# Splitting two stretches of small sample matmuls, a deeper ring of value pages, and finer waits at the first tiles of W_O and W_out

## What is computed

```python
def run_layer(x, c, mix, w_ada, b_ada, g_norm1, w_in, b_forget, g_qa, g_ka, g_qb, g_kb,
              w_o_a, w_o_b, w_out, g_norm2, w_up, w_down):
    mod = (jax.nn.silu(c) @ w_ada + b_ada)[:, None, :]
    shift1, scale1, gate1, shift2, scale2, gate2 = jnp.split(mod, 6, axis=-1)
    h = rms_norm(x, g_norm1) * (1.0 + scale1) + shift1
    qa, ka, va, qb, kb, vb, qi, ki, wi, logf, ga, gb = project(h, w_in, b_forget, g_qa, g_ka, g_qb, g_kb)
    oa, ob = mix(qa, ka, va, qb, kb, vb, qi, ki, wi, logf)
    merged = (jax.nn.sigmoid(ga) * (oa.reshape(B, T, WIDTH_A) @ w_o_a)
              + jax.nn.sigmoid(gb) * (ob.reshape(B, T, WIDTH_B) @ w_o_b))
    x = x + gate1 * (merged @ w_out)
    h2 = rms_norm(x, g_norm2) * (1.0 + scale2) + shift2
    x = x + gate2 * (jnp.square(jax.nn.relu(h2 @ w_up)) @ w_down)
```

```python
    ki_all = jnp.concatenate([paged_rows(cache_k_idx), ki], axis=1)
    scores = index_scores(qi, wi, ki_all, qpos, kpos)
    _, sel = lax.top_k(scores, topk_count(L))
    oa = sparse_attend(qa, gather_selected(cache_k_a, ka, sel), gather_selected(cache_v_a, va, sel), qpos, sel)
```

## Time and profile before

| | |
|---|---|
| median of 3 runs | 951.53 us (951.21 to 955.5) |
| the profiled execution | 950.35 us, its span 948.5 us |
| PE (TensorE matmul) busy | 928.5 us, 98% of the span |
| VectorE, ScalarE, GpSimd busy | 494.1, 396.2, 140.7 us |
| mean granted TensorE clock | 0.994 of full speed |

### The profile page before, as it was taken

One profiled execution on the slowest core, in us unless ns is written; L12 is line 12 of the kernel. 1 busy time (PEld: TensorE's weight loads), 2 busy tenths in 40 slices (PEclk: granted clock), 3 DMA queues, 4 the chain that ended last, 5 costly groups with the idle time before them and its releaser, 6 DMA issues.

```text
span 948.5 us, 19876 instructions
## 1 busy us (share of the span) xinstructions
PE 928.5 (98%) x7554; PEld 852.3 (90%) x7554; DVE 494.1 (52%) x1178; ACT 396.2 (42%) x829; POOL 140.7 (15%) x140
## 2 busy tenths in 40 slices
PE   8999999999999999999999999999999999999997
PEld 7797678787878878997799999999999999999997
DVE  3654678873646797731167576444333344443332
ACT  3354556654756766333233344344211133441111
POOL 4100223222236664200000000000000000000000
PEclk9999999999999999999999999999999999999999
DMA  9648655345325563967233512333323333322212
GB/s 320 212 126 238 188 193 178 91 146 187 106 63 163 166 183 117 294 214 226 76 90 89 157 47 63 88 92 89 89 88 88 91 92 98 96 89 89 88 45 91
DMA packets 176233, 124.54 MB, mean 131 GB/s; under 512 B 14739, under 2 KB 152019, under 8 KB 176164
## 3 DMA queue, kind: packets, MB, share of 16 engines
q1 hardware_dynamic: 176034, 123.50, 43.2%
q10 hardware_dynamic: 130, 0.10, 0.0%
HBM read 116.99 MB, written 6.59 MB: 130 GB/s over the span
## 4 chain that ended last, share of the span: by engine, by line
PE 85%; DVE 5%; issue 4%; ACT 2%; DMA 1%; POOL 1%; SPq 0%; POOLq 0%; ACTq 0%; DVEq 0%
PE bank L975 24%; PE bank L976 23%; PE bank L977 23%; PE bank L1086 2%; PE bank L1063 2%; PE bank L1042 2%; PE bank L1072 2%; PE bank L881 2%; DMA vbuf<-in_cache_v_a 1%; PE bank L1104 1%; PE bank L899 1%; PE bank L1048 1%; PE bank L1127 1%; DVE sel L2006 1%; PE bank L1117 1%
## 5 line engine op out<-in xcount | busy, mean ns | idle before, releaser
L975 PE MATMUL bank<-h_hi,w_hi 128*128 128x256 f32 (+1 forms) x1232 | 359.6, 292 | 1.2 <-issue 0.6
L976 PE MATMUL bank<-h_lo,w_hi 128*128 128x256 f32 (+1 forms) x1232 | 350.2, 284 | 0.0
L977 PE MATMUL bank<-h_hi,w_lo 128*128 128x256 f32 (+1 forms) x1232 | 349.5, 284 | 0.0
L975 PEld LDWEIGHTS bank<-h_hi,w_hi 128*128 128x128 f32 x1232 | 234.2, 190 | 23.7 <-issue 18.9
L976 PEld LDWEIGHTS bank<-h_lo,w_hi 128*128 128x128 f32 x1232 | 234.1, 190 | 0.0
L977 PEld LDWEIGHTS bank<-h_hi,w_lo 128*128 128x128 f32 x1232 | 233.6, 190 | 0.0
L975 PE MATMUL bank<-u_hi,w_hi 128*128 128x264 f32 (+1 forms) x512 | 145.2, 284 | 0.0
L976 PE MATMUL bank<-u_lo,w_hi 128*128 128x264 f32 (+1 forms) x512 | 144.9, 283 | 0.0
L977 PE MATMUL bank<-u_hi,w_lo 128*128 128x264 f32 (+1 forms) x512 | 144.8, 283 | 0.0
L2423 DVE TENSOR_TENSOR w_lo<-raw,w_hi 128x1024 fp32r<-128x1024 f32 x58 | 71.1, 1226 | 132.9 <-ACT w_hi L1762 132.9
L1762 ACT ACTIVATE w_hi<-raw 128x1024 fp32r<-128x1024 f32 x58 | 61.3, 1057 | 139.8 <-PE bank L977 139.8
(11 more groups left out here) (328 smaller groups left out, 1379.0 us busy)
## 6 DMA issues: line engine op xcount, KB each, us to landing
raw<-in_w_in SPq DMA_DIRECT2D x44, 512.0 KB, 4.2
part<-in_w_ada SPq DMA_DIRECT2D x32, 512.0 KB, 5.4
raw<-in_w_up SPq DMA_DIRECT2D x32, 512.0 KB, 4.1
raw<-in_w_down SPq DMA_DIRECT2D x32, 512.0 KB, 4.1
ada<-in_w_ada SPq DMA_DIRECT2D x4, 2048.0 KB, 13.7
kv<-in_cache_k_b SPq DMA_DIRECT2D x16, 256.0 KB, 4.1
qbc<-q_d SPq DMA_DIRECT2D x16, 256.0 KB, 4.5
kv<-in_cache_k_a SPq DMA_DIRECT2D x16, 256.0 KB, 4.4
```

What stands on the lines that cost most here:

```text
L975: mm(out, hi[:, k, :], x_h, start=first and k == ks[0], stop=False)
L976: mm(out, hi[:, k, :], x_l, start=False, stop=False)
L977: end = mm(out, lo[:, k, :], x_h, start=False, stop=last and k == ks[-1])
```

## The change

Five edits. The 16 products of the samples' indexer are cut in two: eight (`first_samples`) stay at slot (3, 6), eight move with `side_step(4)` to slot (3, 7). The ring of value buffers grows from six to eight; the two new ones lie behind everything else that is allocated, fills 6 and 7 wait for nothing, and the fills move in SyncE's program. `sample_outputs` is cut in two: chunks 0 and 1 before the first half of gate tile 15, chunks 2 and 3 between its halves. The first half of the first W_O tile waits only for the first half's evacuation. The first W_out tile waits for chunk 7 only ahead of chunk 7.

```diff
-        (3, 6), (4, 7),
+        (3, 7), (4, 7),
...
-                for j, v_at in enumerate((dist_at, dist_at + 4096, at, at + 4096, at + 8192, kv0_at))]
+                for j, v_at in enumerate((dist_at, dist_at + 4096, at, at + 4096, at + 8192, kv0_at, place["at"], place["at"] + 4096))]
...
-                elif v >= 6:
-                    sp.wait_ge(pv_used, (v - 6) // 4 + 1)
+                elif v >= 8:
+                    sp.wait_ge(pv_used, v // 4 - 1)
                 m, b = batch_unit(v)
-                load_pages(vbuf[v % 6], "cache_v_", m, b, val_landed[v % 6])
+                load_pages(vbuf[v % 8], "cache_v_", m, b, val_landed[v % 8])
...
             load(T_GATE + 14)
+            load_values(6)
+            load_values(7)
             load(T_GATE + 15)
-            for v in range(6, 10):
+            for v in range(8, 12):
                 load_values(v)
             load(T_WO)
-            for v in range(10, 14):
+            for v in range(12, 2 * NS):
                 load_values(v)
             load(T_WO + 1)
             load(T_WO + 2)
-            for v in range(14, 2 * NS):
-                load_values(v)
...
+            def first_samples(p):
+
+                pe.wait_ge(side_read, 4)
+                pe.wait_ge(tok_read, 2 * p + 2)
+                pe.wait_ge(qzs_ready, 1)
+                for i in range(NS * NPAGE // 2):
+                    mm(bank[2][:, H * i:H * i + H], ki_pt[:, i, :], qzs[:, i // 2].rearrange("p c h -> p (c h)"),
+                       start=True, stop=True)
...
                 elif e == 4:
-                    pe.wait_ge(side_read, 4)
-                    pe.wait_ge(qzs_ready, 1)
-                    for i in range(NS * NPAGE):
+                    for i in range(NS * NPAGE // 2, NS * NPAGE):
...
+                if (p, s) == slot_before(*SIDE[4]):
+                    first_samples(p)
...
                 if i == T_GATE + 15:
-                    sample_outputs()
+                    sample_outputs((0, 1))
                 project(i, 0)
+                if i == T_GATE + 15:
+                    sample_outputs((2, 3))
                 project(i, 1)
...
-            pe.wait_ge(os_hi, 1)
-            pe.wait_ge(os_lo, 1)
-            pe.wait_ge(act_evac, act_evac_value(T_WO - 1, 1))
             for g in range(NCH):
...
                 for half in range(2):
+                    if g == 0:
+                        pe.wait_ge(act_evac, act_evac_value(T_WO - 1, half))
+                        if half == 1:
+                            pe.wait_ge(os_hi, 1)
+                            pe.wait_ge(os_lo, 1)
...
+                    out = out_bank(j)[:, 0:CUT[half + 1] - CUT[half]]
+                    if m == 0:
+                        pe.wait_ge(mf_hi, 2 * NCH - 3 + half)
+                        pe.wait_ge(mf_lo, 2 * NCH - 3 + half)
+                        half_tile(i, half, out, range(NCH - 1), last=False)
+                        pe.wait_ge(mf_hi, 2 * NCH - 1 + half)
+                        pe.wait_ge(mf_lo, 2 * NCH - 1 + half)
+                        half_tile(i, half, out, [NCH - 1], first=False).then_inc(proj_done, 1)
+                    else:
+                        half_tile(i, half, out).then_inc(proj_done, 1)
```

More of the change, by code:

```diff
@@ L266, in layer @@
         vbuf = [sb(f"vbuf{j}", [P, NPAGE, SEQ], F32, v_at)[0]
-                for j, v_at in enumerate((dist_at, dist_at + 4096, at, at + 4096, at + 8192, kv0_at))]
+                for j, v_at in enumerate((dist_at, dist_at + 4096, at, at + 4096, at + 8192, kv0_at, place["at"], place["at"] + 4096))]
+        assert place["at"] + 8192 <= nc.sbuf_usable_end
         assert dist_at + 8192 <= abias_at and at + 12288 <= padb_at + 8192
@@ L428, in layer @@
         qbc_landed = [sem("qbc_landed0"), sem("qbc_landed1")]
-        val_landed = [sem(f"val_landed{i}") for i in range(6)]
+        val_landed = [sem(f"val_landed{i}") for i in range(8)]
         prod_pool = sem("prod_pool")
@@ L1249, in sample_values, with sample_outputs @@
                         if pg == 0:
-                            pe.wait_ge(val_landed[v % 6], 16 * NPAGE * (v // 6 + 1))
-                        last = mm(bank[3][32 * j:32 * j + 32, :], ptz[:, 4 * pg + j, 32 * t:32 * t + 32], vbuf[v % 6][:, pg, :],
+                            pe.wait_ge(val_landed[v % 8], 16 * NPAGE * (v // 8 + 1))
+                        last = mm(bank[3][32 * j:32 * j + 32, :], ptz[:, 4 * pg + j, 32 * t:32 * t + 32], vbuf[v % 8][:, pg, :],
                                   start=t == 0 and pg == 0, stop=t == 3 and pg == NPAGE - 1)
                 last.then_inc(pv_used, 1)
-            def sample_outputs():
+            def sample_outputs(cs):
                 pe.wait_ge(om_ready, 2)
-                for c in range(4):
+                for c in cs:
                     out = bank[6][:, 256 + 2 * NS * c:256 + 2 * NS * (c + 1)]
@@ L1263, in sample_outputs @@
                                   start=False, stop=m == 1)
-                last.then_inc(os_done, 1)
+                if c == 3:
+                    last.then_inc(os_done, 1)
             for i in range(T_GATE + 5, T_WO):
@@ L1298, in _ @@
                     i, j = T_WO + NCH + m, NCH * half + m
-                    if m == 0:
-                        pe.wait_ge(mf_hi, 2 * NCH - 1 + half)
-                        pe.wait_ge(mf_lo, 2 * NCH - 1 + half)
                     if half == 0:
@@ L1305, in _ @@
                     pe.wait_ge(dve_evac, 2 * NCH + (j - 3 if j >= 4 else -2 if j < 2 else 0))
-                    half_tile(i, half, out_bank(j)[:, 0:CUT[half + 1] - CUT[half]]).then_inc(proj_done, 1)
+                    out = out_bank(j)[:, 0:CUT[half + 1] - CUT[half]]
[8 more added lines that the diff above has]
+                        half_tile(i, half, out).then_inc(proj_done, 1)
                     if (half, m) == (1, 0):
```

## The result

| | median us | lowest | highest | executions | mean granted clock |
|---|---|---|---|---|---|
| before | 951.99 | 950.42 | 955.50 | 6 | 0.990 to 0.996 |
| after | 943.87 | 939.24 | 945.64 | 6 | 0.995 to 1.000 |

The ratio is 0.9909, with a 95% interval of 0.9891 to 0.9927: faster by 0.9%, 8.1 us by the medians. The forecast was 940.5 us in a range of 937.5 to 944.7, faster. The direction and the range hold; the median lies 3.4 us above the point. (The clocks of before are those of 51 further executions, run beside the experiments.)

The account below looks back on a forecast made before the run. The PE, busy 928.5 of 948.5 us, was taken as the bound, losing time to two clock falls and value-page waits. Terms of 11.07 us gave 939.3 from the profiled 950.35, plus 1.18 for a median: 940.5 us, range 937.5 to 944.7.

Parts of the forecast that it names:

- The products in two slots: Sixteen 8-column products, cut into two stretches of 1.78 us: the clock no longer falls behind them, saving 3.27 us.
- The weakest step: At the split products: a light stretch of 1.78 us keeps the clock, though nothing between 1.95 and 3.34 us was tested.
- `sample_outputs` in two: Around gate tile 15: halves of 1.67 us keep the clock, the half tile behind takes 2.92 us, saving 1.55.
- The ring of eight: Value batches: no wait for pages, each 1.85 us from start to next tile, saving 5.75 us, at least 2.9.
- First W_O tile: Start of W_O: its first half no longer waits for the evacuation of the half just finished, saving 0.80 us.
- W_out: First W_out tile: the relaxed wait costs nothing now, so it saves 0.
- the base: Whole kernel: 1.18 us, the median's distance above the profiled execution, added to 939.3 for a median of 940.5 us.
- the sum: All terms, 3.27 + 5.75 + 1.55 + 0.80 - 0.30 = 11.07 us saved, chance 0.62.
- the upper bounds: Whole kernel: every term at its best, said to be 0.4 us better than the sum.
- The clock falls once more: Rival: a split products or outputs stretch still loses the clock, 942.1 to 943.8 us, chance 0.15; both places 945.3, 0.07.
- Four falls where there were two: Rival: each of four split stretches brings the clock down for 6.83 us; 954.1 us, slower by 0.3%, chance 0.02.
- The ring no longer waits: Answers the rival that one page pair of a value batch is late, losing 2.9 of 5.75 us: 943.4, chance 0.07.

Follow-up runs that it names:

- filled kernels: Kernels with unneeded identity matmuls put into two PE gaps, at 20.4 us and in slot (7, 6); medians from 939.5 to 949.7 us.
- whole_products: After with the sixteen products back in one slot, (3, 6); median 945.09 us, ratio 0.9932.
- add_light8: After with eight 8-column identity matmuls added between the halves of each of gate tiles 10 to 14; median 950.44 us.
- whole_outputs: After with the twelve small matmuls of `sample_outputs` in one piece again before gate tile 15; median 944.32 us, ratio 0.9908.
- ring_only: Before with the ring of eight value pages and nothing else changed; median 948.04 us, ratio 0.9943.
- held_before: Before with identity matmuls filling the PE gaps at 20.4 us and in slot (7, 6); median 949.7 us, ratio 0.9978.
- held_old_wo: held with the old wait, for both halves' evacuation, ahead of the first W_O tile; median 942.77 us.
- held_old_wout: held with the old wait ahead of the first W_out tile; median 940.56 us.
- held: After with six identity matmuls in the PE gap at 20.4 us and seven in slot (7, 6); median 939.5 us, ratio 0.9859.

## Why the prediction was right, and where it was off

**The products in two slots: right.** Both halves take 1.81 us (forecast 1.8) at 1.00. Put back, the fall is back, and the kernel is 3.1 us slower by the medians (3.27 forecast), 3.2 by the means of filled kernels, each with some 2.5 us of play. The price itself varies: 3.27 goes with a fall of 6.83 us, and the fall in the trace of whole_products lasted half of that. The weakest step, that a light stretch of 1.78 us keeps the clock, is borne out by the nine traces with split products; add_light8 has it for 1.70 us. The neighbour has its number now: 2.59 us fails in two of five places.

**`sample_outputs` in two: right in kind, the size varies.** 1.55 us was taken from a fall of 3.42 us. It may last 6.8 (whole_outputs, ring_only), for which twice that is an estimate; undone, the split costs 2.4 us by the medians, give or take 2.5.

**The ring of eight: right.** Every batch takes 1.85 us, no wait of the PE names a value page, and alone the ring gives 4.9 us by the medians, 5.5 by the means. The term of 5.75 was one execution's; held_before's has 4.40.

**First W_O tile 0.80, W_out 0: right**, by the starts in after, held_old_wo and held_old_wout.

**What was off is the base.** "The median of the runs stands 1.18 us above that execution, so for a median I add it". The profile of after stands at 939.24, as the sum has it (939.3), but the median of all twelve executions of after stands 3.5 us above that, at 942.8. The reason is in the first paragraph of the prediction: the clock "is 1.00 everywhere in the body of the program but in two places", read from one execution. In others it falls at the start, for 3.4 to 6.8 us, or in slot (7, 6), behind idle stretches that kept it in that one. Of the nine traces without fills, five show the first and two the second. Before lost 7.2 us to the clock in the mean, where its profile had 10.25 low microseconds, 5.1 lost. That the rest are the same falls is likely rather than shown: ring_only, which has the PE's program of before but for the buffers, has one at the start, and filling both places took 1.9 us off before's mean (951.7 on that chip to 949.8); but a fall behind the outputs of 6.8 instead of 3.4 us would add to it as well. Nothing in the change touches those two places. I had the rows that asked for doubt: each length "is seen once", and three runs of before already spread over 4.3 us. That the median still lies within the range is in part luck: the range had been widened for one fall at a split stretch, and it was falls elsewhere that used the room. (A slip without weight: the upper bounds as written add 0.30 us to the sum, 0.60 if the costs are nothing, and not 0.4.)

In means the account is this. The change gives 9.8 us (952.2 to 942.4) of the 11.07: 4.4 by the clock, forecast 4.82, and 5.4 otherwise, forecast 6.25 (5.75 + 0.80 - 0.30). The 0.85 that is missing of the latter is less than the last column of the table can tell. A ring wait that is shorter in other executions would explain it, and one trace shows such a wait (held_before); ring_only, whose rest is 6.2 us below before's, does not bear it out. A further 0.5 us of the 3.4 is that three runs gave before a median of 951.53, and 51 one of 952.1.

**The rivals.** "The clock falls once more" came out at about the time it named (942.1 to 943.8; after has 943.87, 942.8 over both groups) by another mechanism: in no trace is a fall at a split stretch. Four falls where there were two: none was seen. The ring no longer waits.

## What to carry to other kernels

Look at the mean clock of every execution before you build a sum on one trace: a profile at the fast end of its spread hides falls that the median pays for. Break up or fill stretches in which the PE idles or streams a few columns; six or seven identity matmuls in a gap cost 0 and 0.24 us here, and the five executions of held spread over 1.0 us where six of after spread over 6.4. Then look again: on another chip the filled kernels had a fall at a third place. Judge a wait by the distance between starts, and expect a late transfer to cost another amount next time.

## What the hardware showed that I had not expected

- The same place can keep or lose the clock: idle 1.97 us in slot (7, 6) at 1.00 in after, idle 1.94 us followed by a fall in whole_products; idle 1.40 us and eight 9-column matmuls at the start likewise (a fall in five traces of nine without fills).
- Ahead of the PE's last matmul the fourteen traces have 21 low stretches, in two lengths only, 3.4 and 6.8 us, and the same place showed both (behind the outputs 3.42 in before, 6.8 in whole_outputs).
- The engine need not idle to lose the clock: 2.59 us of 8-column matmuls do it in two of five places, 1.70 us in none of five. 3.63 us of 128-column transposes do not.
- Not all of the spread is the clock: among the fourteen traces the first `mod_turn` starts anywhere from 21.82 to 23.16 us, and in the four filled kernels of the last group, held_before among them, from 22.27 to 22.99, where held had 21.82.
